# Four side sums of GpSimd, two chunks later in each layer's convolved stretch

## The reference

```python
mod = silu(c) @ w_ada[l] + b_ada[l]                # 1024 x 6144: six vectors of 1024
sh1, sc1, gt1, sh2, sc2, gt2 = split(mod, 6)
h = rms_norm(x, norm_mix[l]) * (1 + sc1) + sh1
proj = h @ w_in[l]                                 # q, k, v (3 x 1024), gates, attention, ...
qkv = silu(causal_dwconv(dn_qkv, dn_conv[l]))      # four taps
q, k = l2_norm(q), l2_norm(k)                      # for each head of 128
...                                                # gated delta rule, window attention, merge
x = x + gt1 * (merged @ w_o[l])
...                                                # gated feed-forward with sh2, sc2, gt2
```

## Time and profile before

| | us |
|---|---|
| median of 3 runs | 2391.99 |
| lowest and highest run | 2386.74, 2392.05 |
| profiled execution | 2380.26 |
| its span in the profile | 2378.5 |
| TensorE busy | 2283.2 |
| VectorE busy | 1521.1 |
| ScalarE busy | 1071.8 |
| GpSimd busy | 540.3 |

### The profile page before, as it was taken

One profiled execution on the slowest core, in us unless ns is written; L12 is line 12 of the kernel. 1 busy time (PEld: TensorE's weight loads), 2 busy tenths in 40 slices (PEclk: granted clock), 3 DMA queues, 4 the chain that ended last, 5 costly groups with the idle time before them and its releaser, 6 DMA issues.

```text
span 2378.5 us, 41225 instructions
## 1 busy us (share of the span) xinstructions
PE 2283.2 (96%) x17949; PEld 2190.6 (92%) x17949; DVE 1521.1 (64%) x1826; ACT 1071.8 (45%) x1354; POOL 540.3 (23%) x276
## 2 busy tenths in 40 slices
PE   7998999999999989999999999998999999998999
PEld 7997988899989989898999999878999999878999
DVE  6854676677769256666766655686555655686554
ACT  2653356443345433654344434545344434546433
POOL 0923304499527232046500000000000000000000
PEclk8997999999999979999999999999999999999999
DMA  9751034667657300446655555423555555423553
GB/s 286 247 190 36 1 125 142 213 232 247 213 166 254 130 18 1 159 157 208 205 183 188 175 180 186 150 90 116 186 185 188 175 180 187 150 89 125 182 191 124
DMA packets 332862, 384.22 MB, mean 162 GB/s; under 512 B 12551, under 2 KB 315402, under 8 KB 332554
## 3 DMA queue, kind: packets, MB, share of 16 engines
q1 hardware_dynamic: 332234, 381.42, 49.0%
q10 hardware_dynamic: 448, 0.16, 0.0%
HBM read 380.51 MB, written 1.05 MB: 160 GB/s over the span
## 4 chain that ended last, share of the span: by engine, by line
PE 79%; DVE 11%; ACT 6%; issue 2%; DMA 0%; SPq 0%; ACTq 0%; DVEq 0%
PE bank L697 16%; PE bank L698 15%; PE bank L699 15%; PE bank L920 5%; PE bank L921 5%; PE bank L922 5%; DVE weights_low L1310 4%; ACT weights_high L1985 3%; PE bank L1115 2%; PE bank L1134 2%; PE bank L971 1%; DVE arena L1412 1%; PE bank L711 1%; PE bank L1093 1%; PE bank L983 1%
## 5 line engine op out<-in xcount | busy, mean ns | idle before, releaser
L1310 DVE TENSOR_TENSOR weights_low<-ring,weights_high 128x2048 fp32r<-128x2048 f32 x302 | 743.1, 2461 | 458.0 <-ACT weights_high L1985 457.9
L697 PE MATMUL bank<-h_high,weights_high 128*128 128x256 f32 x3296 | 943.5, 286 | 23.4 <-DVE weights_low L1310 14.2
L698 PE MATMUL bank<-h_low,weights_high 128*128 128x256 f32 x3296 | 928.4, 282 | 0.0
L699 PE MATMUL bank<-h_high,weights_low 128*128 128x256 f32 x3296 | 927.9, 282 | 0.0
L1985 ACT ACTIVATE weights_high<-ring 128x2048 fp32r<-128x2048 f32 x302 | 578.1, 1914 | 705.7 <-PE bank L699 521.6
L697 PEld LDWEIGHTS bank<-h_high,weights_high 128*128 128x128 f32 x3296 | 623.0, 189 | 40.5 <-DVE weights_low L1310 22.3
L698 PEld LDWEIGHTS bank<-h_low,weights_high 128*128 128x128 f32 x3296 | 623.9, 189 | 3.0 <-issue 2.9
L699 PEld LDWEIGHTS bank<-h_high,weights_low 128*128 128x128 f32 x3296 | 623.9, 189 | 0.0
L920 PE MATMUL bank<-hidden_high,weights_high 128*128 128x256 f32 x1056 | 300.3, 284 | 1.3 <-DVE hidden_low L1551 0.8
L921 PE MATMUL bank<-hidden_low,weights_high 128*128 128x256 f32 x1056 | 299.7, 284 | 0.0
L922 PE MATMUL bank<-hidden_high,weights_low 128*128 128x256 f32 x1056 | 299.5, 284 | 0.0
(11 more groups left out here) (409 smaller groups left out, 3101.8 us busy)
## 6 DMA issues: line engine op xcount, KB each, us to landing
ring<-in_w_in SPq DMA_DIRECT2D x80, 1024.0 KB, 5.1
ring<-in_w_up SPq DMA_DIRECT2D x44, 1024.0 KB, 5.3
ring<-in_ffn_w_gate SPq DMA_DIRECT2D x44, 1024.0 KB, 5.2
ring<-in_ffn_w_up SPq DMA_DIRECT2D x44, 1024.0 KB, 5.2
ring<-in_ffn_w_down SPq DMA_DIRECT2D x44, 1024.0 KB, 4.9
side<-in_w_ada SPq DMA_DIRECT2D x42, 1024.0 KB, 7.6
ring<-in_w_down SPq DMA_DIRECT2D x22, 1024.0 KB, 5.0
ring<-in_w_dn_out SPq DMA_DIRECT2D x8, 1024.0 KB, 5.1
```

Source lines behind the costliest of these rows:

```text
L697: mm(o[:, m, :], a_, high[:, t, :], start=(t == 0), stop=False)
L698: mm(o[:, m, :], a_, low[:, t, :], start=False, stop=False)
L699: last = mm(o[:, m, :], b_, high[:, t, :], start=False, stop=(t == KT - 1))
L1310: v.tensor_tensor(low, wide(q), high.bitcast(F32), ALU.subtract).then_inc(chunk_split, 1)
```

## The change

GpSimd's loop squares chunks 0 to 7. Before, a side sum stood ahead of each of the squares of chunks 0 to 3, and the very first of them waited for a small step of VectorE (`d_x`). After, the sums stand ahead of the squares of chunks 2 to 5, and that wait is gone. The side numbers, the sums and their order among each other stay the same. SyncE's queue is not touched.

```diff
             for l in range(LAYERS):
                 for i in range(8):
-                    if l == 0 and i == 0:
-                        pool.wait_ge(d_x, 1)
-                    if i < 4:
-                        side_sum(2 + 24 * l + i)
+                    if i >= 2 and i < 6:
+                        side_sum(24 * l + i)
                     n = 8 * l + i
                     pool.wait_ge(silu_done, 12 * l + i + 1)
```

## The result

The change makes the kernel slower: 2404.12 us, the median of 8 runs (2399.82 to 2410.08), against 2385.86 us for the kernel before, the median of 8 runs beside them. The ratio is 1.0079 with a 95% interval of 1.0063 to 1.0096, which on 2385.86 is +18.8 us (+15.0 to +22.9). The forecast was +15.3 us and 2407, its own range 2402 to 2413.

A forecast was written before the change was run, and what follows sets the result against it. TensorE, busy nearly the whole span, was taken to bound the kernel. First layer 5.6 + 2 and second 5.7 + 2 made 15.3 us, set on the median of 2391.99: 2407 us, range 2398 to 2416 (own range 2402 to 2413).

The forecast's parts named there:

- The chain: Convolved chunks: late sum holds side 4's load until 92.4, chunk 7's ring load behind it; TensorE starts chunk 7 5.6 us later.
- The gain of 1.3 us at chunk 1: First layer: chunk 1's cut, no longer beside a side sum, takes 2.29 us instead of 3.62; bounds 0 and 1.6.
- The start of chunk 7: First layer: TensorE starts chunk 7 at 105.2, where the earlier trace has 99.64.
- the term of 5.6 us: First layer's loss from chunk 7's later start, with the 1.3 us gain already counted.
- The pause: TensorE stands still ahead of chunk 7 in the first layer for 5.6 us.
- The second layer: Same wait at side 28's load; the chunk is cut at 742.0 against a start of 736.29: 5.7 us lost.
- The clock: TensorE at half clock from 102.6 to 109.4, 2.1 us lost; taken as 2 per layer, bounds 0 and 3.4.
- The rival without a fall: Stalls as forecast but TensorE's clock stays at 1.00: +11.3 us, 2403; chance 0.22.
- No second stall: Later side loads, from side 5 on, delay no wanted chunk; chunk 10 is hidden by 2.4 us: cost 0.
- The sum: Both layers' later starts and clock losses together: 15.3 us, giving 2407 us (+0.63%).
- The larger-stalls rival: Both layers: each sum takes 14.3 us, the cut 3.88, and the clock costs more: +24.5 us, 2416; chance 0.12.

The follow-up runs named there:

- e1: The changed kernel with the side loads of the convolved stretch put farther back in SyncE's queue; ratio 1.0006 to the kernel before.
- e2: The kernel before, sums in their old places, with loads of sides 4 and 28 also waiting for the silu of chunk 3; ratio 1.0073.
- e5: The change in the first layer alone, the second layer's sums as in the kernel before; ratio 1.0038.
- e10: The changed kernel with second to fourth sums behind the squares of chunks 4, 5 and 6, and their side loads later; ratio 1.0054.
- e9: The kernel before with the first sum held until chunk 1 is cut, the other three behind all squares, their side loads later; ratio 1.0010.
- e11: The changed kernel measured again, unaltered, against the kernel before; median 2408.93 us, ratio 1.0090.
- e3: The kernel before with each sum one square later, where the change has two; ratio 1.0032.
- e8: The changed kernel with 74 extra matmuls ahead of chunk 7 in each layer, their output unused; ratio 1.0075 to the kernel before.
- e12: The kernel of e8 measured again, beside the changed kernel on the same chip; median 2402.87 us, ratio 1.0069 to the kernel before.
- e4: The changed kernel with 60 extra matmuls ahead of chunk 7 in each layer, their output unused; ratio 1.0116 to the kernel before.
- e6: The kernel before with only GpSimd's first wait, on d_x, taken away; ratio 1.0017.

## Why the prediction was right

**What was late, and who waited.** The chain was forecast link by link, and each link is in the trace: the square ahead of the first sum, the sum, side 4's load, chunk 7 of the ring right behind it, rounding, cut, TensorE, half clock. e1 and e2 show it from both sides: take the queue's wait away and the 10.5 us of a stretch become 0.7 (2.2 with what lies behind it), though all sums are moved; add only the wait and most of the loss comes, though GpSimd's program is the old one. e5 shows that each layer gives half.

**The gain of 1.3 us at chunk 1** came: the cut takes 2.29 us, not 3.62. TensorE starts chunk 1 at 64.37, not 65.45, although the stretch begins 0.5 us later.

**The start of chunk 7** was forecast for 105.2 and came at 107.90, so the term of 5.6 us was mis-sized: it is 8.3 against the earlier trace rows. Link by link, in the first layer: the silu ended at 79.3 rather than 79.0 (+0.3); the square took 1.98, not 1.04 (+0.9); the sum 12.3, not 12.4 (-0.1); side 4 took 0.41 to issue, not 0.58 (-0.2); chunk 7 took 7.95 to land, not 7.7 (+0.25); the cut took 3.86, not 2.6 (+1.25). With some 0.2 between the links that is the 2.7. Two links make most of it. For the cut I had both ends, 2.29 and 3.88, and chose 2.6 because "its own row of today" had 2.54; but the change moves both the cut and the sum beside it, and the old row says nothing of the new company. e10 shows what company costs: cut 2.29, pause 1.2 to 1.5 us shorter. The square had only been seen alone, and got no upper end. It begins under a cut of VectorE that ends at 80.41, and ends 0.91 us behind it:

```profile
79.34 1.98 POOL L2390 TENSOR_TENSOR arena<-arena 128x512 f32<-128x512 f32 x1 [2.81 <-ACT arena L2034]
```

```profile
78.12 2.29 DVE L1310 TENSOR_TENSOR weights_low<-ring,weights_high 128x2048 fp32r<-128x2048 f32 x1 [0.48 <-ACT weights_high L1985]
```

So it is in the other traces: squares begun under a running cut take 1.97 or 1.98 us (e1, e9, e10, e11), in e3 even 3.09 at 738.43 under a cut that ends at 740.61; squares begun with no cut running take 1.04. It could have been read ahead: today's cut runs from 79.21 to 81.51, and the silu that starts the square ends at 80.3.

**The pause** was put at 5.6 us, the shift of the start. It is 8.9: 8.3, and the time by which TensorE was done earlier, thanks to the gain at chunk 1.

**The second layer** was mis-sized in the same way: 41.97 us from the copy of the keys to chunk 7 before (736.29 - 694.32), 50.05 after (761.65 - 711.60), so 8.1 where I had 5.7.

**The clock.** The forecast had it fall 3.0 us behind the stop, with 4.2 us of half clock on work and 2.1 lost. The first layer has just that: 98.97 to 102.0, and 107.90 to 112.1. In the second the stop is at 752.72, the fall at 757.35 (the slice at 757 has 0.65) and the end at 767.5 (the slice at 767 has 0.73), so 5.9 us on work and 2.9 lost. e8 and e12 price it from the other side, 1.5 to 1.9 us a layer by the stretches. The rival without a fall is excluded: the slices show 0.50.

The Trainium skill (TensorE: Matmul & The Clock Gate, Why this matters for your kernels) warns of half clock behind idle gaps between bursts; the change shows it behind 8.9 us. e3 and e4 show it behind 3.1 and 1.8 us as well.

**No second stall.** Costed at 0, and it was: TensorE's other waits in the two stretches sum to 2.4 and 1.5 us (11.3 - 8.9 and 10.4 - 8.9), no more than before. Of the first layer's rest, 0.45 us is a wait at 127.62 for a cut of 3.88 us beside a sum. The terms: 8.3 of later start, less 0.5 for the later copy of the keys, plus 2.1 of clock, make 9.8 of the 10.5 us by which the stretch grew. In the second layer 8.1 and 2.9 make 11.0 against the 10.8 measured.

**The sum.** Stretches +10.5 and +10.8, together 21.3 against the forecast's 15.3. Measured: +18.8 (15.0 to 22.9), in e11 +21.5 (1.0090 on 2387.53). The forecast's 2407 came out 3 us above the measured 2404 although its difference was too small by 3.5 to 6, because I set it on the median of three runs (2391.99), and more runs of the kernel before gave 2383 to 2388. That the time fell so near is partly luck: two errors of opposite sign. The larger-stalls rival (+24.5) was nearer than the forecast by the stretches and farther by the whole runs: its long cut came, its sums of 14.3 us did not (12.3 and 8.3 us for the first two).

**What lies outside the stretches stays open.** In the profiled executions the part between the two stretches took 558.5 us before, 564.8 in the change, 564.9 in e11, 563.2 and 563.8 in e8 and e12, 558.5 in e10. Adding up the shortfall of the granted clock over slices of 10 us of this part (length times one less the clock) gives 22.0 us before, 27.3 in the change, 27.2 in e11, 27.4 in e8 and e12, 20.3 in e10. So by this sum most of the 6.3 us is time at half clock. It can be seen where the delta rule is prepared, slices of 2 us, first of the kernel before and then of the changed one at the same work:

```profile
186.00:188.00 2.00, 2.00 (x18) 2.00 (x18) 0.79 (x1) 0.00 (x0) 2.00 (x3) 0.90 0.00 0
188.00:190.00 2.00, 2.00 (x12) 2.00 (x11) 0.00 (x0) 0.00 (x0) 2.00 (x3) 0.50 0.70 202
190.00:192.00 2.00, 2.00 (x12) 1.79 (x12) 0.20 (x1) 0.00 (x0) 1.75 (x2) 0.74 0.91 319
```

```profile
198.00:200.00 2.00, 2.00 (x10) 2.00 (x11) 0.00 (x0) 0.00 (x0) 2.00 (x3) 0.50 0.00 0
200.00:202.00 2.00, 2.00 (x12) 2.00 (x11) 0.00 (x0) 0.00 (x0) 2.00 (x3) 0.50 0.88 242
202.00:204.00 2.00, 2.00 (x11) 2.00 (x11) 0.00 (x0) 0.00 (x0) 0.77 (x1) 0.50 0.80 282
```

The instructions are the same; half clock lasts longer after the change. It repeats in e11, and this is also where e10's 6.4 us are. What decides how long it lasts I cannot say: no run moves this part by itself. Nor does it follow the stall, for e8 has none and loses as much, and e6, which has none either, took 563.2 us here with a shortfall of 23.9, so 4.7 us more for only 1.9 of shortfall. Each of these numbers is from a single execution, and the medians do not have to follow: the profiled execution of before lies 5.6 us below its median, that of the change 5.9 above.

## What to carry to other kernels

In SyncE's queue the wait for side 4 held everything behind it, whatever that was for (chunk 7 left 12.5 us later). Before moving a producer later, find the loads that wait for it, and what is queued behind those: a consumer with slack can stand ahead of a load without any. If the producer has to be late, move its load back in the queue too (e1: one list of places took away all but some 4 of the 21 us in the two stretches). And measure to a point behind everything that was moved, or a cost that has only been pushed back looks like none. Where an instruction may or may not have company from another engine, take the old row for its duration only if the company stays the same.

## What the runs showed of the hardware that I had not expected

The clock falls behind shorter pauses than I had thought, and not always: in e4 it went to 0.68 and 0.50 behind a pause of 1.83 us in the first layer and held through one of 1.8 us in the second; in the kernel before it held through 2.21 us; in e3 it fell behind 3.1 us, in e1 behind 2.01 and in e9 behind 2.49. The length of the pause alone does not tell these apart.

GpSimd can hold up short instructions of VectorE more than long ones in proportion: scalings of 0.48 us took 1.5 to 2.6 us beside a side sum (e6), while a cut of 2.29 us took 3.85. The Trainium skill (SBUF — State Buffer, Who interferes with whom) has the two exclude each other for whole instructions, by which a short one would wait for the whole long one ahead of it; 2.1 to 2.6 us beside L2375, of which two together take 4.01 us there, agree with that. It goes the other way as well: the square of 1.04 us, begun under a cut, took 1.98 and ended 0.91 us behind the cut's end, and the L2376 of 2.4 us took 4.35.
